# State-space stage of a two-block layer: decay rows broadcast by split fp32r products, squares added on VectorE before their sum

## What is computed

```python
def ssd_scan(xs, dt, a_neg, bm, cm, h0):
    ...
    acum = jnp.cumsum(loga, axis=2)
    a_t = jnp.moveaxis(acum, 2, -1)
    seg = a_t[..., :, None] - a_t[..., None, :]
    lmat = jnp.exp(jnp.where(causal, seg, -jnp.inf))
    cb = jnp.einsum('bcqgn,bcsgn->bcgqs', cmc, bmc)
    y_diag = jnp.einsum('bcgrqs,bcsgrp->bcqgrp', cb[:, :, :, None] * lmat, xdt)
    ...
    y_off = jnp.einsum('bcqgn,bcgrpn->bcqgrp', cmc, h_prev) * jnp.exp(acum)[..., None]
def ssd_out_norm(y, z, w):
    yg = (y * jax.nn.silu(z.astype(jnp.float32))).reshape(bsz, L, SSD_GROUPS, SSD_WIDTH // SSD_GROUPS)
    yg = yg * lax.rsqrt(jnp.mean(yg * yg, axis=-1, keepdims=True) + EPS)
```

## Time and profile before

| | |
|---|---|
| time before, median of 3 (all three) | 3851.46 us (3850.87, 3851.46, 3862.23) |
| the profiled execution, its own time | 3850.77 us |
| its span, from first to last instruction | 3849.0 us |
| TensorE matmul busy | 3646.1 us (95%) |
| VectorE / ScalarE / GpSimd busy | 1978.1 / 1508.4 / 441.2 us |
| mean granted TensorE clock | 0.979 |

### The profile page before, as it was taken

How to read it: one execution, slowest core, us unless ns; L and a number is a source line. 1 busy time by engine, 2 the same in 40 slices (tenths; PEclk the granted TensorE clock), 3 DMA queues, 4 the chain that set the end, 5 groups by cost and what they waited for, 6 DMA issues and landing times. The chain is left out here.

```text
span 3849.0 us, 52548 instructions
## 1 busy us (share of the span) xinstructions
PE 3646.1 (95%) x21192; PEld 3073.2 (80%) x21192; DVE 1978.1 (51%) x3090; ACT 1508.4 (39%) x2513; POOL 441.2 (11%) x350
## 2 busy tenths in 40 slices
PE   6999999999888789999999999999999999999997
PEld 3688888788666778888888778888899888878886
DVE  6555555466656634755555554446533444453453
ACT  3322222255455443555565532324322444442332
POOL 1000000134211000010111140120000000032021
PEclk7999999999999899999999999999999999999999
DMA  9643322322543445422233153347866767643332
GB/s 349 238 150 129 118 98 85 105 84 61 177 114 89 107 146 160 129 83 85 81 94 89 53 177 96 96 85 108 125 122 114 120 94 115 104 108 101 88 99 88
DMA packets 590179, 448.55 MB, mean 117 GB/s; under 512 B 64390, under 2 KB 520530, under 8 KB 588656
## 3 DMA queue, kind: packets, MB, share of 16 engines
q1 hardware_dynamic: 581744, 421.18, 43.3%
q10 hardware_dynamic: 6048, 19.14, 1.2%
q0 software_dynamic: 2144, 4.87, 0.4%
HBM read 387.61 MB, written 57.46 MB: 116 GB/s over the span
## 5 line engine op out<-in xcount | busy, mean ns | idle before, releaser
L2069 DVE TENSOR_TENSOR w_lo<-w,w_hi 128x512 fp32r<-128x512 f32 x428 | 291.9, 698 | 532.4 <-ACT w_hi L2062 532.3
L2062 ACT ACTIVATE w_hi<-w 128x512 fp32r<-128x512 f32 x428 | 262.0, 626 | 518.0 <-PE od_acc L2048 184.0
L4032 DVE TENSOR_TENSOR w_lo<-w,w_hi 128x512 fp32r<-128x512 f32 x260 | 206.5, 797 | 392.0 <-ACT w_hi L3939 390.5
L3909 PE MATMUL ta_acc<-ta_x_hi,w_hi 128*128 128x512 f32 x960 | 376.3, 392 | 6.4 <-ACT ta_embed L3960 3.2
L3910 PE MATMUL ta_acc<-ta_x_lo,w_hi 128*128 128x512 f32 x960 | 374.7, 390 | 0.0
L3911 PE MATMUL ta_acc<-ta_x_hi,w_lo 128*128 128x512 f32 x960 | 374.7, 390 | 0.0
L3939 ACT ACTIVATE w_hi<-w 128x512 fp32r<-128x512 f32 x260 | 163.8, 631 | 490.3 <-PE ta_acc L3911 458.6
L2046 PE MATMUL od_acc<-od_u_hi,w_hi 128*128 128x512 f32 x768 | 304.4, 396 | 1.8 <-DVE od_u_lo L2712 1.8
L2048 PE MATMUL od_acc<-od_u_hi,w_lo 128*128 128x512 f32 x768 | 299.3, 390 | 0.0
L2047 PE MATMUL od_acc<-od_u_lo,w_hi 128*128 128x512 f32 x768 | 299.1, 389 | 0.0
L2046 PE MATMUL ev_acc<-ev_u_hi,w_hi 128*128 128x512 f32 x608 | 251.6, 414 | 13.6 <-DVE ev_u_lo L2831 4.6
(11 more groups left out here) (701 smaller groups left out, 8470.7 us busy)
## 6 DMA issues: line engine op xcount, KB each, us to landing
w<-in_o_w_in_dram SPq DMA_DIRECT2D x260, 256.0 KB, 7.3
p_w<-in_w_in_dram SPq DMA_DIRECT2D x72, 512.0 KB, 6.2
w<-in_e_w_in_dram SPq DMA_DIRECT2D x144, 256.0 KB, 3.0
mod_w<-in_w_ada_dram SPq DMA_DIRECT2D x32, 1024.0 KB, 11.9
w<-in_ple_gate_w_dram SPq DMA_DIRECT2D x128, 256.0 KB, 2.8
gate_w<-in_w_ada_dram SPq DMA_DIRECT2D x16, 1024.0 KB, 6.2
z_w<-in_w_in_dram SPq DMA_DIRECT2D x64, 256.0 KB, 2.9
w<-in_e_w_out_dram SPq DMA_DIRECT2D x64, 256.0 KB, 2.8
```

The costliest lines, as they stand in the source:

```text
L2062: act.activation(self.w_hi[m % self.ring][:], self.w[m % self.ring][:], ACT.Copy).then_inc(self.hi_set, 1)
L2069: eng.tensor_tensor(self.w_lo[m % self.ring][:], self.w[m % self.ring][:], self.w_hi[m % self.ring][:].bitcast(F32), ALU.subtract).then_in ...
L3909: pe.matmul(bank, hi, hi_x[:, k, :], start=(k == 0), stop=False)
L4032: dve.tensor_tensor(w_lo[m % RING][:], w[m % RING][:], w_hi[m % RING][:].bitcast(F32), ALU.subtract).then_inc(lo_set, 1)
```

## The change

The broadcast takes two fp32r products in place of one fp32 product. For it VectorE makes, once in each group and behind the last state addition, a rounded copy `cum_hi` of the cumulated logs, the rest `cum_lo`, and an fp32r copy of the identity. TensorE waits for all three before mask 0 (ahead also of the projection steps that are due before that mask). The three tiles lie in SBUF bytes that `x_w` and what follows it use, so GpSimd waits in group 1 until all masks of group 0 are made. In the norm, VectorE adds blocks 2 and 3 of the squares to 0 and 1, then 1 to 0, and TensorE sums the one block that is left.

```diff
+        with ExitStack() as after_adds:
+            ident_r, cum_hi, cum_lo = (after_adds.enter_context(nc.sbuf_tensor("ssd_" + nm, [P, *shape], F32R)) for nm, shape in (
+                ("ident_r", (P,)), ("cum_hi", (LC, 2, SSD_H)), ("cum_lo", (LC, 2, SSD_H))))
@@ tensor: expo_sums
                 for i in range(4):
-                    last = pe.matmul(bank[EXPO_BANK[n % 4]][:, i * P:(i + 1) * P],
-                                     heads(3, c + CTX_CHUNKS, d, g, 4 * half + i, 1).to_broadcast([P, P]), ident[:], start=True, stop=True)
+                    h = g * HPG + 4 * half + i
+                    out = bank[EXPO_BANK[n % 4]][:, i * P:(i + 1) * P]
+                    pe.matmul(out, cum_hi[:, c, d, h:h + 1].to_broadcast([P, P]), ident_r[:], start=True, stop=False)
+                    last = pe.matmul(out, cum_lo[:, c, d, h:h + 1].to_broadcast([P, P]), ident_r[:], start=False, stop=True)
@@ tensor: after the ten additions of group g
+                pe.wait_ge(cum_lo_set, 2 * (g + 1))
                 for n in range(4):
                     expo_sums(g, n)
@@ tensor: norm
-                pe.wait_ge(squares, g + 1)
-                for b in range(GB):
-                    last = pe.matmul(bank[2][:, :], ones[:], y_sq[:, b, :], start=(b == 0), stop=(b == GB - 1))
-                last.then_inc(sums, 1)
+                pe.wait_ge(added, 2 * (g + 1))
+                pe.matmul(bank[2][:, :], ones[:], y_sq[:, 0, :], start=True, stop=True).then_inc(sums, 1)
@@ gpsimd: head of group g
+                if g > 0:
+                    pool.wait_ge(cum_ready, MASKS * g)
@@ vector: after the ten additions of group g
+                dve.tensor_copy(cum_hi[:], tabs[:, 3, CTX_CHUNKS:CHUNKS]).then_inc(cum_hi_set, 1)
+                dve.tensor_copy(ident_r[:], ident[:]).then_inc(cum_lo_set, 1)
+                dve.wait_ge(cum_hi_set, g + 1)
+                dve.tensor_tensor(cum_lo[:], tabs[:, 3, CTX_CHUNKS:CHUNKS], cum_hi[:].bitcast(F32), ALU.subtract).then_inc(cum_lo_set, 1)
@@ vector: norm
+                dve.wait_ge(squares, g + 1)
+                dve.tensor_tensor(y_sq[:, 0:2, :], y_sq[:, 0:2, :], y_sq[:, 2:4, :], ALU.add).then_inc(added, 1)
+                dve.wait_ge(added, 2 * g + 1)
+                dve.tensor_tensor(y_sq[:, 0, :], y_sq[:, 0, :], y_sq[:, 1, :], ALU.add).then_inc(added, 1)
                 dve.wait_ge(inv_set, g + 1)
```

More of the change, by code:

```diff
@@ L2345, in ssd_stage @@
         z_set, z_out_set = sem("z_set"), sem("z_out_set")
+        cum_hi_set, cum_lo_set, added = sem("cum_hi_set"), sem("cum_lo_set"), sem("added")
         block = ctx.enter_context(nc.Block())
```

## The result

The changed kernel takes 3864.11 us (median of 20 runs, 3855.32 to 3871.16) against 3851.95 (20 runs, 3847.05 to 3862.23) before: ratio 1.0029, 95% interval 1.0023 to 1.0036. The forecast was 3862. It is a small loss, 12.2 us between the medians, but the interval lies clear of 1. The profiled execution took 3864.49 us, its span 3861.9.

The account below looks back on a forecast made before the run. TensorE, busy 95% of the span, was taken as the bound. Broadcast 0, wait +5.8, norm -1.1 and clock +7 sum to +11.7 us on 3850.77, so 3862 us, range 3848 to 3871.

Parts of the forecast that it names:

- The broadcast: Mask products on TensorE: weight load sets each record at 0.112 us, so eight records still take 0.89 us; 0 change.
- The rival by the Trainium skill's count of passes: Broadcast: two split passes replace four fp32 ones, halving 28.6 us, -14.3 us; taken up in the moving-side rival, chance 0.11.
- The wait before mask 0: TensorE stops 2.9 us in each group for VectorE's last addition and three small tiles; together +5.8 us.
- The norm: Norm of each group: fewer TensorE products against VectorE's added additions, -0.55 us each, -1.1 us in all.
- The clock: Half clock after four TensorE stops: 1.5 us for each before the masks, 2.0 for each in the norm; +7 us.
- term 0: The broadcast's term in the sum: two fp32r products per head cost the same as before, 0 us.
- The clock holds: Rival for the whole stage: the stops cost only themselves, giving 3855.5 us, no change; chance 0.12.
- Two records: Rival for the broadcast: each fp32r product runs as two records, 512 in all, 28.6 us more, 3891 us; chance 0.07.
- Moving side: Rival for the broadcast: moving columns set the price, -13.8 us, mask to mask 1.85 us, 3849 us in all; chance 0.11.
- GpSimd's new wait: GpSimd's wait in group 1 for group 0's masks: costs nothing, since its next work needs transposes made after those masks.

Follow-up runs that it names:

- split-only: The changed kernel with the norm as before: 3867.38 us, ratio 1.0040; run again 3866.03 us, ratio 1.0036.
- the kernel kept busy: The changed kernel with TensorE doing products of no use in the four stops: 3853.08 us, ratio 1.0006 against before.
- norm only: The kernel before with only the norm's additions: 3854.73 us, ratio 1.0009; with TensorE kept busy in the norms, 3846.55 us, ratio 0.9986.
- the hi product alone: Split broadcast with tiles made early and no wait, norm as before, each head's low product left out: 3843.52 us, ratio 0.9978 against before.
- norm filled: The kernel before with the norm's additions, and projection steps in place of busy products in the norm's wait; fp32 masks: 3839.31 us, ratio 0.9970.

## Why the prediction was right

**The broadcast: 0, as predicted.** The record count (256), the spacing (0.11 us) and mask to mask (2.28 us) came as the one-column products of the earlier trace rows told, and leaving a product out took off its 0.11 us. The Trainium skill, page "TensorE: Matmul & The Clock Gate", section "LDWEIGHTS (loading the stationary operand)", has the load go by the number of weight columns over 1.2 GHz, by which 128 columns are an estimate of 107 ns. The trace agrees at full clock, with 0.11 us for 128 weight columns and 0.06 for 64. At half clock the split records start 0.21 us apart (as at 915.96 and 916.17 us in the second split-only profile), so what sets the spacing takes about twice as long there. The rival by the Trainium skill's count of passes, page "FP8 and Floating Point Precision", section "TensorE Precision Notes", falls for 128 moving columns: by that count two passes stand in place of four, and mask to mask stayed at 2.28 us.

**The wait before mask 0: +5.8 predicted, 5.3 found.** The small copies took 218 ns and the subtraction 281, close to the 230 and 290 interpolated from the earlier trace rows. The overlap of the bars is larger than I took: the addition's bar ends at 773.89 and the last tile at 774.36, 0.47 us later and not 0.7. From bar to bar the stop is 2.44 us; in effect, by the kernel kept busy, it costs 2.7 and 2.6.

**The norm: -1.1 predicted, -1.1 and -1.2 found** in the two kernels that keep the clock up, the changed one and norm only.

**The clock: +7 predicted, 11.4 in this execution: the term that was mis-sized.** I priced each stop by what followed stops elsewhere: 1.5 us for each stop before the masks, 2.0 for each in the norm. Three of them came near, with 1.6 before group 0's masks and 2.3 and 2.8 in the norms. It failed for the one ahead of group 1's masks: 4.7 us, from 10.2 us of half clock here and 17.1 and 20.5 in the split-only profiles. The length of half clock after a stop is not the stop's alone: it depends on what TensorE does next, and the split itself changed that work. Nor did any of these stops go free, as one in the earlier trace rows had: half clock followed all ten stops of 2.4 us in the five profiles that have them. So the split was not free, as my term 0 had it: with the waits in place it costs 3866.03 - 3860.37 = 5.7 us more than fp32 masks behind the same waits. Both were run side by side on one chip.

The sum came within 2.1 us of the median, helped by luck: in the profiled execution +5.3 - 1.1 + 11.4 = +15.6 for this stage, with 0.1 more in its start (measured 321.4 - 305.6 = 15.8), against 11.7 forecast, and the rest of the program, which the change doesn't touch, was 2.9 us shorter than before.

**The rivals.** "The clock holds" (3855.5): what the kept-busy kernel shows (3853), but not what happened. "Two records": refuted by the count. "Moving side": refuted twice, by mask to mask of 2.28 us and by 1.84 with the hi product alone. GpSimd's new wait cost nothing, as said: the last mask of group 0 is made at 829 us, and GpSimd works on group 0 until 840.

## What to carry to other kernels

Price a small product by the spacing of its records, and look for the term that sets it: with 128x128 fp32 or fp32r weights a record cost 0.11 us here at full clock with 128 fp32r columns, 128 fp32 ones or, for fp32, a single one, so halving the streaming of a 128-column product gained nothing. In a stage that TensorE bounds, an edit that makes TensorE wait must pay for the wait and for the clock behind it; fill the wait with steps that are due anyway (norm filled: 0.3%, though its profile accounts for a third of that), and if it can't be filled, put 512-column products behind it (here six steps, for 3.4 us of half clock in place of 20.5). Where splitting an operand needs small tiles first, make them long before they are needed, in bytes that are idle then.

## What the runs showed that I had not expected

After equal stops of 2.4 us the half clock lasted 3.4 us ahead of fp32 masks or dense projection steps, and 10.2, 17.1 and 20.5 us ahead of split masks with one projection step between them; at full clock the same masks ran through 61 us without a fall. Dense steps did not always end it after 3.4 us: in the norm of group 1 of the changed kernel it lasted 6.8, with two records of the norm and then projection steps in it. TensorE's busy time fills all the rows of the masks, at either clock, so that column of the profile does not tell whether a stretch will bring the clock back.
